# A decoder step: the low-rank products of the time mixer taken from inputs that are not yet normed

## What is computed

```python
xn = rms_norm(h, prm['mix_norm'][i])
x_prev = jnp.concatenate([shift_prev[:, None, :].astype(x.dtype), x[:, :-1]], axis=1)
xs = x[None] + (x_prev - x)[None] * mu[:, None, None, :]
r, k, v = jnp.einsum('nbtd,nde->nbte', xs[:3], w_rkv)
xv, xw, xa, xg = xs[2], xs[3], xs[4], xs[5]
w = -jax.nn.softplus(-(w0 + jnp.tanh(xw @ w1) @ w2).astype(jnp.float32)) - 0.5
a = jax.nn.sigmoid(a0 + (xa @ a1) @ a2)
```

## Time and profile before

| | us |
|---|---|
| median of 3 runs | 1601.19 |
| lowest, highest | 1600.58, 1601.4 |
| the profiled execution, in all | 1601.69 |
| its span, first to last instruction | 1600.1 |
| TensorE busy in the span | 1563.8 (98%) |
| VectorE busy | 974.6 (61%) |
| ScalarE busy | 688.5 (43%) |
| GpSimd busy | 95.8 (6%) |

### The profile page before, as it was taken

How to read it: one execution, slowest core, us unless ns; L and a number is a source line. 1 busy time by engine, 2 the same in 40 slices (tenths; PEclk the granted TensorE clock), 3 DMA queues, 4 the chain that set the end, 5 groups by cost and what they waited for, 6 DMA issues and landing times.

```text
span 1600.1 us, 34795 instructions
## 1 busy us (share of the span) xinstructions
PE 1563.8 (98%) x14400; PEld 1472.0 (92%) x14400; DVE 974.6 (61%) x1539; ACT 688.5 (43%) x1048; POOL 95.8 (6%) x129
## 2 busy tenths in 40 slices
PE   7999999998999999999999999999999999999998
PEld 7999997997888899999999999999777769999998
DVE  6655437686896575554458555545767766655532
ACT  4443324563655553333353434333355544433421
POOL 0000000002322200000001430000000000000000
PEclk9999998999999999999999999999999999999999
DMA  7444452430100554444445454446779993444442
GB/s 234 159 151 139 143 174 77 139 126 16 30 17 10 160 184 140 148 151 145 152 132 193 146 162 156 132 156 231 247 292 388 373 339 111 154 138 155 151 146 79
DMA packets 207199, 255.02 MB, mean 159 GB/s; under 512 B 17858, under 2 KB 188114, under 8 KB 206946
## 3 DMA queue, kind: packets, MB, share of 16 engines
q1 hardware_dynamic: 203426, 247.64, 46.0%
q0 software_dynamic: 3648, 5.57, 1.4%
HBM read 246.84 MB, written 6.35 MB: 158 GB/s over the span
## 4 chain that ended last, share of the span: by engine, by line
PE 90%; DVE 6%; ACT 2%; DMA 1%; issue 1%; SPq 0%; DVEq 0%
PE ps L723 23%; PE ps L724 23%; PE ps L725 23%; PE ps L1018 4%; PE ps L1013 3%; PE ps L1359 3%; PE ps L1448 2%; PE ps L775 1%; DVE ring_r L2035 1%; PE ps L1044 1%; PE ps L1443 1%; PE ps L1153 1%; PE ps L1169 1%; PE ps L1108 1%; DMA ring<-in_ffn_w_in 1%
## 5 line engine op out<-in xcount | busy, mean ns | idle before, releaser
L723 PE MATMUL ps<-arena_r,ring_r 128*128 128x320 f32 (+1 forms) x2016 | 625.8, 310 | 0.1
L725 PE MATMUL ps<-arena_r,ring_r 128*128 128x320 f32 (+1 forms) x2016 | 623.2, 309 | 0.0
L2035 DVE TENSOR_TENSOR ring_r<-ring,ring_r 128x2048 fp32r<-128x2048 f32 (+1 forms) x130 | 291.3, 2242 | 252.7 <-ACT ring_r L1565 147.4
L723 PEld LDWEIGHTS ps<-arena_r,ring_r 128*128 128x128 f32 x2016 | 379.9, 188 | 4.0 <-issue 3.0
L725 PEld LDWEIGHTS ps<-arena_r,ring_r 128*128 128x128 f32 x2016 | 379.9, 188 | 0.0
L724 PE MATMUL ps<-arena_r,ring_r 128*128 128x320 f32 x1136 | 351.0, 309 | 0.0
L724 PE MATMUL ps<-xn_r,ring_r 128*128 128x320 f32 (+2 forms) x880 | 272.3, 309 | 0.0
L724 PEld LDWEIGHTS ps<-arena_r,ring_r 128*128 128x128 f32 x1136 | 213.3, 188 | 0.2
L2035 DVE TENSOR_TENSOR arena_r<-arena,arena_r (+3 forms) x155 | 141.9, 926 | 111.7 <-ACT arena_r L1565 49.6
L1565 ACT ACTIVATE ring_r<-ring 128x2048 fp32r<-128x2048 f32 (+1 forms) x70 | 128.3, 1834 | 128.5 <-DMA ring<-in_ffn_w_out 89.4
L723 PE MATMUL ps<-arena_r 128*128 128x320 f32 x592 | 183.2, 309 | 0.0
(11 more groups left out here) (365 smaller groups left out, 1879.2 us busy)
## 6 DMA issues: line engine op xcount, KB each, us to landing
ring<-in_ffn_w_in SPq DMA_DIRECT2D x67, 1024.0 KB, 5.0
arena<-in_cache_v SPq DMA_DIRECT2D x64, 512.0 KB, 6.5
ring<-in_cache_k SPq DMA_DIRECT2D x64, 512.0 KB, 5.9
ring<-in_ffn_w_out SPq DMA_DIRECT2D x24, 1024.0 KB, 5.1
arena<-in_ffn_w_in SPq DMA_DIRECT2D x21, 1024.0 KB, 5.0
ring<-in_rw_w_rkv SPq DMA_DIRECT2D x11, 1024.0 KB, 5.2
ring<-in_ffn_w_out SPq DMA_DIRECT2D x12, 768.0 KB, 4.4
arena<-in_ffn_w_out SPq DMA_DIRECT2D x8, 1024.0 KB, 5.1
```

The lines of the kernel that those rows point to most:

```text
L723: pe.matmul(out, part(s, 1)[:, k, cs], x_hi, start=first_, stop=False)
L725: return pe.matmul(out, part(s, 0)[:, k, cs], x_hi, start=False, stop=last)
L2035: return TT(out, x, high.bitcast(F32), ALU.subtract)
```

## The change

The product with the weights and the norm's scale for each token can change places, since the scale is the same for all features of a token. The changed kernel multiplies `wa1` and `wa1_mu` by h scaled with the norm's gain alone (`raw_in`), and applies each token's scale to the 128 x 320 results.

- **ScalarE** writes `raw_in` tile by tile in the last part of ffn0 (`raw_input`), and copies the spread reciprocals to SBUF (`rs`) and both products (`lora_sum`, `lora_prev`). Small activations on one element load the tanh and the sigmoid tables ahead of their use. The high parts of k's inputs are taken in pieces (2, 3, 3) between these.
- **TensorE** runs the eight matmuls of the first product around the norm's small steps (3, 2, 1, 2), then eight of 328 columns for the second one: the 8 columns behind the tokens are the incoming shift rows, unscaled, in `raw_in`.
- **GpSimd** scales both products by `rs`, subtracts them and adds the second one shifted by a token, six operations.
- **VectorE** makes xn and df in two halves, with the first mixed inputs between them; the second half reads the scale from `rs`.
- **The low-rank outputs** are two groups of eight tiles, one behind k.0 and one in the middle of k.1 (between its two banks); ScalarE takes the high half of slab k.2 between the two groups of sigmoids.

```diff
-    add("rms_mix0", 1)
-    add("wa1", 1, "a")
+    add("rms_mix0", 1, "a")
+    add("wa1", 2, "a")
     add("k.0", 2)
-    add("wa2", 2 * DT, "a")
-    for q in range(1, 4):
+    add("wa2_0", DT, "a")
+    add("k.1", 1)
+    add("wa2_1", DT, "a")
+    add("k.1b", 1)
+    for q in range(2, 4):
...
-                 (tile_done, first["wa2"] + 2 * DT))
+                 (tile_done, first["wa2_1"] + DT))
...
+            def lora_raw(*ks):
+
+                for k in ks:
+                    pe.wait_ge(S("raw_in"), k + 1)
+                    mm = pe.matmul(bank(lora, T), wa1[:, k, :], raw_in[:, k, 0:T], start=(k == 0), stop=(k == DT - 1))
+                return mm
...
+            end(lora_raw(6, 7))
+            begin(lora + 1)
+            pe.wait_ge(S("lora_scaled"), 2)
+            dve_done(first["shift_in"])
             for k in range(DT):
...
+                mm = pe.matmul(bank(lora + 1, TX), wa1_mu[:, k, :], raw_in[:, k, :], start=(k == 0), stop=(k == DT - 1))
             end(mm)
...
+            lora_out(0)
+            mixed_gemm("k", 1, between=lambda: lora_out(1))
+            mixed_gemm("k", 2, 3)
...
+            def raw_input(m):
+                act.activation(raw_in[:, m, 0:T], h[:, m, :], ACT.Copy, scale=prm("mix_norm", m)).then_inc(S("raw_in"), 1)
...
+            high_inputs("k", range(0, 2))
+            filled(lora + 1)
+            act.activation(lora_prev, bank(lora + 1, TX), ACT.Copy).then_inc(act_freed, 1)
+            high_inputs("k", range(2, 5))
+            act.wait_ge(S("lora_summed"), 3)
+            act.activation(lora_sum[0:HD, :], lora_sum[0:HD, :], ACT.Tanh).then_inc(S("lora_tanh"), 1)
+            act.activation(fstat[:, 0, 0:1], eps, ACT.Sigmoid)
+            high_inputs("k", range(5, DT))
             for m in range(DT):
+                if m == 4:
+                    hi(first_slab["k"] + 2)
...
-            k_out(0)
+            k_out(0, 1)
             lo(first_slab["k"] + 2)
+            k_out(2)
             for m in range(DT):
                 mixed_low("r", m)
-            k_out(1)
+            k_out(3)
...
+            pool.wait_ge(act_freed, freed["a"][first["wa1"] + 2])
+            pool.tensor_tensor(lora_prev[:, 0:T], lora_prev[:, 0:T], rs[:, :], ALU.mult).then_inc(S("lora_normed"), 1)
+            pool.tensor_tensor(lora_sum, lora_sum, rs[:, :], ALU.mult).then_inc(S("lora_normed"), 1)
+            pool.wait_ge(S("lora_normed"), 2)
+            pool.tensor_tensor(lora_sum, lora_sum, lora_prev[:, 0:T], ALU.subtract).then_inc(S("lora_normed"), 1)
+            pool.wait_ge(S("lora_normed"), 3)
+            for to, x in ((lora_sum[:, 1:TP], lora_prev[:, 0:TP - 1]), (lora_rest[:, :, 1:QS], prev_rest[:, :, 0:QS - 1]),
+                          (lora_rest[:, :, 0], lora_prev[:, T:TX])):
+                pool.tensor_tensor(to, to, x, ALU.add).then_inc(S("lora_summed"), 1)
```

More of the change, by code:

```diff
@@ L894, in _, with mixed_gemm, lora_out @@
                           start=True, stop=True))
-            t = first["wa1"]
-            begin(t)
-            pe.wait_ge(S(f"slab{LORA}"), low_rank[1])
+            end(lora_raw(6, 7))
+            begin(lora + 1)
+            pe.wait_ge(S("lora_scaled"), 2)
+            dve_done(first["shift_in"])
             for k in range(DT):
[L900 to L906, removed]
-            end(mm)
-            def mixed_gemm(name, *parts):
-                gemm(name, xs_hi[name], AR_(mix_buf[name]), (S("xs_split"), "krv".index(name) * DT), parts=parts)
-            mixed_gemm("k", 0)
[L913 to L919, removed]
+                mm = pe.matmul(bank(lora + 1, TX), wa1_mu[:, k, :], raw_in[:, k, :], start=(k == 0), stop=(k == DT - 1))
+            end(mm)
+            def mixed_gemm(name, *parts, between=None):
+                gemm(name, xs_hi[name], AR_(mix_buf[name]), (S("xs_split"), "krv".index(name) * DT), parts=parts,
+                     between=between)
+            def lora_out(half):
+                pe.wait_ge(S("lora_tanh"), 1)
+                for m in range(4 * half, 4 * half + 4):
+                    for e, pr in enumerate((slice(0, HD), slice(HD, P))):
+                        t = lora_tile(m, e)
+                        begin(t)
+                        end(pe.matmul(bank(t, T), wa2[pr, m * P:(m + 1) * P], lora_sum[pr, :], start=True, stop=True))
+            mixed_gemm("k", 0)
+            lora_out(0)
+            mixed_gemm("k", 1, between=lambda: lora_out(1))
+            mixed_gemm("k", 2, 3)
             pe.wait_ge(S("shift_cols"), 1)
@@ L1557, in _ @@
         def _(act):
+            lora = first["wa1"]
             def filled(t):
@@ L2076, in mixer_norm, with normed @@
                 filled(first["shift_in"])
[L2077 to L2084, removed]
+                free(CP(shT, bank(first["shift_in"], DT * BS).rearrange("p (m b) -> p m b", m=DT)))
+                filled(first["rms_mix0"])
+            def normed(ms, rms):
+                for m in ms:
+                    STT(xn[:, m, :], h[:, m, :], prm("mix_norm", m, 0), rms, ALU.mult, ALU.mult
+                        ).then_inc(S("xn_raw"), 1)
+                dve.wait_ge(S("xn_raw"), ms[-1] + 1)
             def ffn(n):
@@ L2247, in key_sums @@
                 free(TS_(rs[:, :], bank(first["kk_norm"], T), 1e-24, None, ALU.max))
-            dve.wait_ge(S("df_ready"), 2)
-            mixed_input("k")
+            normed(range(0, 4), bank(first["rms_mix0"], T))
+            shifted(slice(0, 4))
+            dve.wait_ge(S("df_ready"), 1)
+            for m in range(4):
+                mixed_raw("k", m)
+                if m >= 2:
+                    mixed_low("k", m - 2)
+            dve.wait_ge(act_freed, freed["a"][first["rms_mix0"] + 1])
+            normed(range(4, DT), rs[:, :])
+            mixed_low("k", 2)
+            mixed_low("k", 3)
+            shifted(slice(4, DT))
+            dve.wait_ge(S("df_ready"), 2)
+            for m in range(4, DT):
+                mixed_raw("k", m)
+                if m >= 6:
+                    mixed_low("k", m - 2)
+            mixed_low("k", DT - 2)
+            mixed_low("k", DT - 1)
             lo(first_slab["k"] + 1)
```

63 lines of the change are left out of this document (43 added, 20 removed).

## The result

| | before | after |
|---|---|---|
| median of ten runs, us | 1601.36 | 1606.41 |
| lowest, highest | 1599.57, 1606.08 | 1604.53, 1612.84 |
| the profiled execution, in all | 1601.69 | 1605.16 |
| its span | 1600.1 | 1603.5 |

A forecast was written before the change was run, and what follows sets the result against it. TensorE is busy 98% of the span, but VectorE was taken as co-critical up to the first copy of k's banks. That copy 4.1 us late, less 0.4 us, gave +3.7 us: 1604.9 us, range 1599.5 to 1608.3.

The forecast's parts named there:

- N: Moment of VectorE's first normed tile, 255.63 us before; forecast to move by +0.2 us, bounds -0.3 and +3.3.
- Self-wait: VectorE's eight norm tiles split four and four: same work, one more self-wait, +0.15 us.
- X: Moment of VectorE's first copy of k's banks, 275.96 us in the profile before.
- ScalarE's order: Tanh, table load and small activation ahead of high 5 make VectorE wait: +1.25 us, bounds 0 and 2.0.
- GpSimd, +2.5: Six GpSimd operations exclude VectorE instructions reading two SBUF tiles: VectorE loses 2.5 us, bounds 0 and 3.1.
- Rival A: Exclusion between GpSimd and VectorE costs nothing: 1602.4 us; chance 0.18.
- X': VectorE's first copy of k's banks in the changed kernel: forecast at 280.06 us, 4.1 us late.
- From X' to k.2: Stretch from the first copy of k's banks to k.2's start: forecast -0.4 us, bounds -1 and +1.5.
- Half clock in k.0: TensorE waits some 4 us in k.0, then runs at 0.30 us a matmul; hidden under VectorE, costing nothing.
- Rival C: Half clock falls when k.1 begins: 24 slow matmuls cost 3.5 us more, +7.2, 1608.4 us; chance 0.17.
- K: Milestone: the start of k.2 on TensorE; the forecast carries its shift through to the end unchanged.
- E: Milestone used for reading the profiles: the start of the last matmul of ffn0.

The follow-up runs named there:

- first profile of before: The first of two profiled executions of the unedited kernel before, the one the prediction was made from; 1601.69 us.
- after, first: The first of four profiled executions of the unedited changed kernel; 1605.16 us.
- without GpSimd: Changed kernel without its six GpSimd operations and ScalarE's wait for them; one run, 1607.08 us.
- high parts first: Changed kernel with ScalarE taking high parts 5 to 7 ahead of the tanh and the sigmoid table load; 1607.52 us, ratio 1.0041.
- before, filled: Kernel before with three unread matmuls in TensorE's idle stretch ahead of the column sums; 1602.54 us, ratio 1.0007.
- scale from PSUM: Changed kernel with the second four norm tiles reading the scale from the PSUM bank instead of SBUF; 1605.22 us, ratio 1.0024.

## Why the prediction held, step by step

1604.9 us was forecast, with a range of 1599.5 to 1608.3, and 1606.41 was measured. Slower by over 0.2% had the largest chance. The mechanism was the forecast's; the size was short by 1.5 us, of which 0.2 is the base (a median of 1601.36 in ten runs, where 1601.19 was used).

- **N, +0.2.** Measured +0.29 against the first profile of before, with the full clock, as expected. But from the column sums to N it took 4.17 us (251.62 to 255.79) and the profile that I had took 3.86, nearly all at the half clock. With the clock kept, before takes 2.53: then the three matmuls in that path cost 1.6 us. That half-clock stretch was read as a property of the kernel, and it was one of that execution. This is the term of the sum that was mis-sized: +0.3 to +1.6 depending on the execution.
- **Self-wait, +0.15.** Not separated. The three terms between N and X together were 23.85 - 20.33 = 3.52 for a forecast of 3.9.
- **ScalarE's order, +1.25.** 0.99 us of wait in the row, 1.06 when it was undone. Above my lower bound, near the value taken. The small activation stands 0.01 us behind the load (270.43 + 1.28, and 271.72). The drain that the Trainium skill (ScalarE: Activation LUTs, What ACT_TABLE_LOAD costs) adds to a switch is not seen here.
- **GpSimd, +2.5.** 2.31 us in the row, 2.29 when left out. The six themselves ran from 261.99 to 266.98, 5.0 us for an estimate of 2.6 to 3.1 alone. Rival A is refuted.
- **X' 280.06.** 279.64.
- **From X' to k.2, -0.4.** Measured 0.0 against the first profile (11.36 and 11.39), +0.4 against the second (10.96). k.1 began at X' + 1.7 rather than 1.4, and the second group of outputs, four pairs, took 2.36 us (285.02 to 287.38) where I had some 2.0. The gate itself was as drawn: the copy of k.1's first bank ends 6.85 us behind X', for 6.9, and no wait for it shows in the row of the second outputs.
- **Behind k.2.** From k.2's start to r's first matmul it is 14.87 us in all six profiles of the two kernels: k.3's slab cost nothing, as forecast. The next slab load, its high and its low half answer 3.64, 3.46 and 3.46 us later, in the chain of waits:

```profile
298.23 5.16 DMA ring<-in_rw_w_rkv
303.41 1.92 ACT ring_r L1598
305.36 2.29 DVE ring_r L2086
```

- **Half clock in k.0, hidden.** It came in all four profiles of the changed kernel (265.8 to 272.6 in the first), and X - N is the same to 0.01 us in all four. Hidden indeed, and smaller than forecast: a matmul took 0.27 us for 0.30 and the full clock was back before k.0 ended, so that k.0 ended at 275.70 for 278.3. That left the hole of 2.59 us ahead of the fourth pair, where the forecast had 0.5.
- **Rival C, 0.17.** "It decides if the idle stretch just ahead of X' is longer than the 1.76 us seen before." It was 2.59 in the first profile with no fall of the clock, and 1.54 in the second with one. The price was too high as well: 1.5 to 1.6 us in each of the three profiles that show it (K - X of 12.90 to 12.93 for 11.36), not 3.5, since a matmul took 0.27 us and not 0.30, and the clock was back after 3.4 us. A threshold on the length of one hole was the wrong condition, and rival C is not another outcome of the kernel but a share of its executions.
- **Sum.** The forecast was +3.7 us at K; between the first two profiles it is 3.8 from E, and 3.4 in the span. For the 5.05 us of the medians the six profiles offer two reasons: a base that is 1.76 us shorter in one of two, and 1.9 us more in one of four of the changed kernel. The mean of K - E is 41.9 and 36.8, 5.1 apart. That fits, but with so few profiles it is argued and not shown. In the same six executions the times differ by 6.4 us on the average, 1.1 of it behind K, and that part varies by 4.4 us between single executions (1312.5 to 1316.9). Its share stays open.

## What to carry to other kernels

Filling a hole in the engine that is busy 98% gained nothing here, because the engine it next waits for had unbroken work: a start of k.0 that was 6.2 us earlier ended in waits for VectorE (3.45, 0.39 and 2.59 us) and in half clock, while VectorE's own path grew by 3.5 us. Work given to an idle GpSimd is paid by VectorE if VectorE reads two SBUF tiles at that time (2.3 us here); give VectorE a PSUM operand there, or move the GpSimd work. And where a profile shows a stretch at half clock on a path that a change touches, take a second profile before using its durations as a base.

## What the runs showed of the hardware

- The same program with the same idle stretch of 1.76 us had its clock at 0.50 from 0.35 us behind that stretch in one execution (252.1), and in another only from 3.5 us behind it (254.3), with a second idle stretch of 0.73 us ending at 254.04. It stayed there for 10.2 us in the one and 3.4 us in the other. After 2.59 us idle the clock stayed at 1.00 (after, first) or fell (without GpSimd). Where it falls varies from execution to execution.
- Time gained just ahead of a wait can be lost, mostly to the clock: 2.29 us at X (without GpSimd), 1.06 (high parts first) and 1.34 at N (before, filled) had become 0.65, -0.49 and 0.11 us at K. It need not be: 1.17 us at X (scale from PSUM) were 1.18 at K, in an execution whose clock stayed at 1.00 from 276 us to K.
- A SCALAR_TENSOR_TENSOR on VectorE with one input in PSUM runs beside GpSimd at full speed (1.92 us for four), with both in SBUF it takes 4.23 us for four beside GpSimd and 1.93 without.
